# A two-layer decoder trunk on one core: mixer tails reordered, gathers in fp32r for two experts at a time, products on zeros

## What is computed

```python
h = rmsnorm(x, ln_attn[l])
proj = h @ w_in
o_a = nsa_mixer(q, k_c, v_c, k_s, v_s, k_w, v_w, gl, ...)   # attention: compressed, selected, window
o_b = conformer_conv(conv_in, ...)                          # 31 taps, layer norm, silu, @ conv_pw
o_c = retention(rq, rk, rv, rg, ret_gn)
x = x + concat([o_a, o_b, o_c]) @ w_out
h = rmsnorm(x, ln_ffn[l])
if l == 0: x = x + swiglu(h, ffn_w13, ffn_w2)               # dense, D_FF 2816
else:      x = x + moe_ffn(h, router, moe_w13, moe_w2)      # 8 experts, 2 per token
return rmsnorm(x, ln_final)                                 # after both layers
```

## Time and profile before

| | us |
|---|---|
| median of 3 runs (lowest, highest) | 1372.23 (1370.99, 1373.15) |
| the profiled execution, its own time | 1370.95 |
| its span, first to last instruction | 1369.1 |
| first mixer, dense layer, second mixer with routing, experts: start on PE | 0, 191.8, 378.9, 571.4 |

### The profile page before, as it was taken

The page is one execution under the profiler, slowest core; times in us unless marked ns, Lnnn a source line. Parts: engine busy times, 40 slices in busy tenths (PEclk is TensorE's granted clock), DMA queues, the critical chain, the costliest instruction groups (busy, mean ns, idle before and its releaser), DMA issues.

```text
span 1369.1 us, 16238 instructions
## 1 busy us (share of the span) xinstructions
PE 1304.7 (95%) x6341; PEld 1044.3 (76%) x6341; DVE 986.0 (72%) x1119; ACT 828.0 (60%) x1194; POOL 3.8 (0%) x10
## 2 busy tenths in 40 slices
PE   6998979999999988799999999999999999999997
PEld 5867548888888764588878878878888888888785
DVE  2476255544425753598998998898998998988986
ACT  2125344444311353587887787787787787778785
POOL 0000000000000000000000000000000000000000
PEclk9999999999999999899999999999999999999999
DMA  7205266552520340698988988988898898898881
GB/s 323 109 9 204 110 253 242 192 191 82 220 104 11 142 179 8 271 382 353 366 342 343 367 341 344 367 353 329 348 375 338 330 390 339 332 389 336 337 350 50
DMA packets 32913, 357.66 MB, mean 261 GB/s; under 512 B 3776, under 2 KB 3904, under 8 KB 5312
## 3 DMA queue, kind: packets, MB, share of 16 engines
q1 hardware_dynamic: 32832, 356.56, 66.9%
HBM read 355.49 MB, written 1.05 MB: 260 GB/s over the span
## 4 chain that ended last, share of the span: by engine, by line
PE 88%; DVE 8%; ACT 3%; issue 1%; DMA 0%; DVEq 0%; ACTq 0%
PE ps L565 84%; PE ps L568 3%; DVE wlU L1616 3%; DVE x L1748 1%; ACT whU L1183 1%; DVE arena L1449 0%; ACT arena L1096 0%; DMA x<-x_in 0%; DVE x L1583 0%; DVE arena L1634 0%; DVE hT L1373 0%; ACT gTh L1209 0%; ACT L1158 0%; ACT L1135 0%; DVE xn L1603 0%
## 5 line engine op out<-in xcount | busy, mean ns | idle before, releaser
L1616 DVE TENSOR_TENSOR wlU<-ring,whU 128x2048 fp32r<-128x2048 f32 x198 | 453.2, 2289 | 64.7 <-ACT whU L1183 59.3
L1183 ACT ACTIVATE whU<-ring 128x1024 fp32r<-128x1024 f32 x396 | 418.4, 1061 | 65.0 <-PE ps L565 60.5
L565 PE MATMUL ps<-whU,hTh 128*128 128x512 f32 x880 | 353.0, 401 | 4.1 <-DVE wlU L1616 4.1
L565 PE MATMUL ps<-whU,hTl 128*128 128x512 f32 x880 | 345.0, 392 | 0.0
L565 PE MATMUL ps<-wlU,hTh 128*128 128x512 f32 x880 | 343.0, 390 | 0.0
L1623 DVE TENSOR_TENSOR wlD<-ring,whD 128x2048 fp32r<-128x2048 f32 x97 | 222.0, 2289 | 62.2 <-ACT whD L1195 62.2
L1195 ACT ACTIVATE whD<-ring 128x1024 fp32r<-128x1024 f32 x194 | 205.3, 1065 | 83.3 <-PE ps L565 78.7
L565 PEld LDWEIGHTS ps<-whU,hTh 128*128 128x128 f32 x880 | 165.3, 188 | 37.4 <-DVE wlU L1616 6.1
L565 PEld LDWEIGHTS ps<-whU,hTl 128*128 128x128 f32 x880 | 165.1, 188 | 36.1
L565 PEld LDWEIGHTS ps<-wlU,hTh 128*128 128x128 f32 x880 | 166.1, 189 | 32.5
L565 PE MATMUL ps<-whD,gTh 128*128 128x512 f32 x428 | 169.0, 395 | 0.0
(11 more groups left out here) (193 smaller groups left out, 977.2 us busy)
## 6 DMA issues: line engine op xcount, KB each, us to landing
ring<-moe_in SPq DMA_DIRECT2D x88, 2048.0 KB, 8.2
ring<-moe_in SPq DMA_DIRECT2D x88, 1024.0 KB, 8.4
ring<-ffn_in SPq DMA_DIRECT2D x11, 2048.0 KB, 7.7
ring<-mix_in SPq DMA_DIRECT2D x6, 3072.0 KB, 10.6
ring<-ffn_in SPq DMA_DIRECT2D x11, 1024.0 KB, 7.4
ring<-mix_in SPq DMA_DIRECT2D x4, 2048.0 KB, 13.1
ring<-mix_in SPq DMA_DIRECT2D x2, 2176.0 KB, 8.5
ring<-mix_in SPq DMA_DIRECT2D x2, 2112.0 KB, 13.5
```

The source lines that it names most:

```text
L565: return nc.tensor.matmul(o, lhsT, rhs, start=first, stop=last, skip_group_check=True)
L1183: A(whU[:, p, :], ring[:, f.slot(J), p * PIECE:(p + 1) * PIECE], ACT.Copy).then_inc(s_hi, 1)
L1616: V.tensor_tensor(wlU[:, w, :], raw, whU[:, w, :].bitcast(F32), ALU.subtract).then_inc(s_lo, 1)
```

## The change

- `HEAD`: `vsw` 1 goes behind `rqk` 0; `kcv` 0 goes ahead of `score` 0 and `kcv` 1 ahead of `score` 1, with the taps of the convolution on DVE placed anew.
- `BESIDE`: `convB` and `conv_pw` go from ahead of `pv` 6 and `cmpkv` to the next unit, behind `score` 9 and `retcat`; `cscore` goes ahead of `out` 0.
- `TAIL`: `pre` 0 goes ahead of `pv` 11 and `pre` 1 behind `attn_sum` 1; `out_rest` 2 ahead of the first `xT`. DVE's add to `x` moves from `xT` to `out_rest`. `kT` moves in the arena, so that the pieces written early hold nothing that is still read.
- Dense step 0 runs all four weight pairs for token tile 0, then for tile 1.
- The tokens are split in two fp32r parts (`xh` by ACT, `xl` by DVE) in place of three bf16 parts; `pick` is fp32r for two experts, 256 columns; a gather is made for experts 0, 2, 4, 6 only, in four banks, and the odd expert's share is stored in j = 1 of the even one. Scatter goes to j = 2, its adds to j = 3.
- The router's products go behind the last `xT`, all together.
- PE multiplies zeros: 30 products ahead of the first norm, 14 ahead of the rank counts, 8 ahead of the first gather. ACT loads the Sqrt table at the start.

```diff
-HEAD = [("stat", 0), ("nT", 0), ("stat", 1), ("vsw", 0), ("nT", 1), ("vsw", 1), ("rqk", 0), ("rqk", 1),
+HEAD = [("stat", 0), ("nT", 0), ("stat", 1), ("vsw", 0), ("nT", 1), ("rqk", 0), ("vsw", 1), ("rqk", 1),
...
-       [("ks", 0)] + conv(7, 10) + [("score", 0), ("kcv", 0)] + conv(10, 11) + [("score", 1), ("kcv", 1)] + conv(11, 12)
+       [("ks", 0)] + conv(7, 9) + [("kcv", 0), ("score", 0), ("kcv", 1)] + conv(9, 11) + [("score", 1)] + conv(11, 12)
...
-          6: [("roots", 0), ("hidT", 0), ("hidT", 1), ("cnorm", 1), ("rsilu", 0), ("convB", 0), ("retnorm", 1)],
-          7: [("conv_pw", 0), ("cmpkv", 0)], 8: [("retcat", 0), ("out", 0), ("cscore", 0)], 9: [("out", 1)],
+          6: [("roots", 0), ("hidT", 0), ("hidT", 1), ("rsilu", 0), ("cnorm", 1), ("retnorm", 1)],
+          7: [("convB", 0), ("cmpkv", 0), ("retcat", 0), ("conv_pw", 0)], 8: [("cscore", 0), ("out", 0)], 9: [("out", 1)],
...
-TAIL = [("out_rest", 0), ("attn_sum", 1), ("out_rest", 1), ("pre", 0), ("xT", 0), ("out_rest", 2), ("pre", 1),
-        ("xT", 1), ("xT", 2), ("out_rest", 3), ("xT", 3)]
+TAIL = [("out_rest", 0), ("attn_sum", 1), ("pre", 1), ("out_rest", 1), ("out_rest", 2), ("xT", 0), ("xT", 1),
+        ("out_rest", 3), ("xT", 2), ("xT", 3)]
...
+            def keep_busy(o, n):
+                for _ in range(n):
+                    mm(o[:, 0:T], warm[:, 0:P], warm[:], True, True)
...
             def dense():
-                for J in range(STEPS):
+                for i in range(NT):
+                    for p in range(UP):
+                        up(DENSE, 0, p, 0, i)
+                for J in range(1, STEPS):
...
+                for part, (src, made) in enumerate(((xh, s_xh), (xl, s_xl))):
+                    pe.wait_ge(made, NT)
+                    for c in range(KD):
+                        for i in range(NT):
+                            last = mm(ps[:, GATHER[c // 2], (c % 2) * 2 * P:(c % 2 + 1) * 2 * P],
+                                      src[:, i, c * P:(c + 1) * P], pick[:, i, :], c % 2 == i == part == 0,
+                                      i == NT - 1 and part == 1)
...
-                    last = mm(ps[:, 3, i * P:(i + 1) * P], pick[:, i, :], identb[:], True, True)
+                    last = flip(ps[:, 3, i * P:(i + 1) * P], pick[:, i, (ex % 2) * P:(ex % 2 + 1) * P].bitcast(F32))
...
-                    if j == 1 and e:
+                    if j == 2 and e:
                         scatter(ex - 1)
...
-                    if j == 7 and e < EXPERTS - 1:
+                    if j == 7 and ex % 2 and e < EXPERTS - 1:
                         gather(ex + 1)
...
+            pe.wait_ge(s_warm, 1)
+            keep_busy(ps[:, 0, :], 30)
             mixer(0)
...
                     elif stage == "pre":
                         f = MOE[0] if l else DENSE
                         if k == 0:
-                            full(act, l, "attn_sum", 1)
+                            full(act, l, "score", len(UNITS) - 1)
                             act.preload_act_table(ACT.Sqrt)
+                        else:
+                            full(act, l, "pv", len(UNITS) - 1)
...
+                    if j == 1 and ex % 2 == 0:
+                        picked(ex + 1)
```

More of the change, by code:

```diff
@@ L882, in up @@
                                      k == 0, k == KD - 1)
-                last.then_inc(s_piece, 1)
+                if only != 0:
+                    last.then_inc(s_piece, 1)
             def turn(f, J):
@@ L1023, in _ @@
             mixer(1)
-            logits(1, 1)
+            pe.wait_ge(s_late, 32)
+            for i in range(NT):
+                for h in range(2):
+                    logits(i, h)
+            keep_busy(ps[:, RANK, :], 14)
             pe.wait_ge(s_sel, 1)
@@ L1320, in _ @@
             mixer(1)
-            for i in range(NT):
-                act.wait_ge(s_xr, i + 1)
-                A(xb[1][:, i, :], xn[:, i, :], ACT.Copy).then_inc(s_xb, 1)
             act.wait_ge(s_m1, 2)
@@ L1578, in mixer @@
                         lo_up(MOE[0] if l else DENSE, 0, k)
-                    elif stage == "xT":
+                    elif stage == "out_rest":
                         i, h = divmod(k, 2)
```

128 lines of the change are left out of this document (65 added, 63 removed).

## The result

| | before | after |
|---|---|---|
| median of 4 runs (lowest, highest) | 1371.76 (1370.99, 1373.15) | 1353.80 (1352.98, 1354.18) |
| profiled execution, its span | 1370.95, 1369.1 | 1353.87, 1352.0 |
| ratio of the times, 95% interval | | 0.9867 (0.985 to 0.9884) |

The change saves 18.0 us by the medians and 17.1 by the profiled executions; 18.1 were forecast. The sum was right, several of its terms were not. The table compares the prediction's terms with what the two traces give; the measured column is the growth of the lead at PE's landmarks, so it also holds what a term hands on to the next stage. The second mixer is counted from the transposes ahead of its first projection (375.98 before, 369.95 after).

The account below looks back on a forecast made before the run. PE, busy 95% of the span, was taken as the bound. From 1370.95 us, -1.4 - 1.0 - 2.6 + 4.2 - 4.9 - 5.4 - 7.0 = -18.1 gave 1352.9, rounded to 1353; range 1344 to 1363.

Parts of the forecast that it names:

- Gathers: Experts: four fp32r gathers of 32 products at 0.12 us each in place of eight bf16 ones; -7.0 us.
- load and stream don't overlap: Expert gathers: rival that weight load and stream run in turn, 0.225 us a product, +13, 1366; chance 0.10.
- plain f32 rate: Expert gathers: rival that fp32r at 256 columns takes 0.44 us a product, +41, 1394; chance 0.04.
- DVE becomes the bound: Even experts: rival that the odd expert's `picked` work costs 2.3 us in four of them, +9, 1362; chance 0.10.
- Head and scores: Both mixers' starts: heads -1.4 and -1.0; `kcv` 0 filling PE's wait before the scores, -1.3 twice.
- PE comes warm: First mixer's head: PE's first projection runs faster, 16 records in 3.9 us in place of 5.82.
- Middles: Middle of each mixer: PE idles about five us ahead of `conv_pw` and the clock falls; +2.1 twice.
- the clock holds: Middles and tails: rival that the clock doesn't fall, 1.8 back at each of four places, -7, 1346; chance 0.12.
- First tail: First mixer's tail to dense start: dense layer starts 5.7 us sooner, its late weight pieces cost +0.8; -4.9.
- But the splits are then done: First mixer's tail: weight splits are finished when PE's wait for `attn_sum` 1 ends; `out_rest` 1 then ends at 176.5.
- Second tail and routing: Second mixer's tail to first expert: first expert starts sooner, -5.4 us, or -1.6 if products on zeros don't hold the clock.
- the router's 32 records at 557.3 (0.11 each): Routing after the second mixer's last `xT`: router products take 0.11 us each and end at 557.3.

Follow-up runs that it names:

- the run with halves: The changed kernel with each 256-column gather product issued as two of 128 columns on the same stationary operand; 1367.25 us, ratio 0.9966.

## Why the prediction was right, step by step

- **Gathers, forecast -7.0, measured -8.2: right in its mechanism.** 0.119 us a product where 0.12 was taken, and the run with halves shows 0.112 as the floor below 256 columns; that it is the weight load is the likeliest reading, not shown. Two terms were mis-sized. Turning `pick` by f32 transposes was put at +0.8 in all: in the chain of expert 0 the step with them takes 8.47 us (598.33 to 606.80) and took 8.43 with the bf16 products, so 0.3 in all. And the second step behind a gather takes some 0.25 more than others (8.47 before, 8.51 now, against 8.23); behind the first gather there were seven such steps and are three, -0.8 where the sum had nothing. With -7.9 for the gathers and a new wait of 0.43 in expert 0, at 583.94, that makes -8.0. The rivals "load and stream don't overlap", "plain f32 rate" and "DVE becomes the bound" are excluded: an even expert takes 95.70 us and an odd one, which has the gather, 99.76, so the even one has no 2.3 us more.
- **Head and scores, forecast -5.0, measured -4.8.** Taken back, the order of the head costs 4.2, and the zeros at the start 1.1 to 1.7. The late weights make PE wait 0.84, forecast 1.0. Within the sum the first head gave 0.6 more, and the scores 1.0 less: PE now waits 0.74 in each mixer ahead of `pv` 0 (at 88.33 in the first), where 0.3 was taken. The forecast's "PE comes warm" was true of the profiled execution, not of most others with these zeros.
- **Middles, forecast +4.2, measured +4.45.** Gap, place, clock and cause were as written, and undoing them gave 4.9. The rival "the clock holds" is wrong.
- **First tail, forecast -4.9, measured -5.0: right number, wrong reason.** The step "But the splits are then done" says that the early splits make it short. The old list on the new code costs only 0.55 there and about 1 in step 0; and splits *behind* the products make it 4.3 shorter still. What gave 5.5 us is the addition to `x` in `out_rest`: the first one no longer stands behind a split, PE's waits shrink by 2.3, and the clock holds where two slow stretches cost 3.4. The prediction used this order but gave it no price.
- **Second tail and routing, forecast -5.4, measured -3.5.** The step "the router's 32 records at 557.3 (0.11 each)" failed: they take 5.80 us, as the clock falls under them. It was at 1.00 until 548 and at 0.50 from 549 on; before that, PE was busy 0.76 of the 2.00 us from 545 to 547 (the wait of 1.51 ahead of `xT` 3 is there). The zeros bring the clock back, but only in the gather, and are worth 1.25 and not 3.8.
- The misses have both signs: experts -1.2, first head -0.6, second tail and routing +1.9, scores +1.0. That the sum is right to 1 us by the profiled executions, and to 0.1 by the medians, is partly luck.

## What to carry to other kernels

When all engines walk one list, ask of each entry who waits behind it on each engine: the best moves here cost nothing but an order (`conv_pw` and `out` 0 behind work that needs nothing of ACT, 6.4 + 2.3 us over both mixers), and the same list is wrong for a stage in which ACT and DVE have a norm to make too (-4.3 us in one mixer, +1.7 in the other). Before a group of operations is split to fit a gap, look for the reader or the bank that waits for its *last* member. And a term that comes out right should still be undone in parts: the first tail's was, and its cause was another edit. Last, look at the same stretch in more than one trace before you credit it to an edit: the quick first records of the changed kernel were seen in two of twelve.
